# Fetching the first two experts' tokens by rows in a two-layer encoder on one core

## The reference

```
def expert_choice_moe(h, w_router, w_gate, w_up, w_down):
    aff = softmax(xt @ w_router)                 # 256 tokens x 16 experts
    gate, idx = top_k(aff.T, cap)                # cap = 32 tokens per expert
    xe = take(xt, idx, axis=0)
    hid = silu(xe @ w_gate) * (xe @ w_up)        # 1024 -> 1024, per expert
    ye = (hid @ w_down) * gate
    out = zeros_like(xt).at[idx].add(ye)
```

## Time and profile before

| | us |
|---|---|
| median of 3 runs | 1794.33 |
| profiled execution, in all | 1795.57 |
| its span | 1793.8 |
| PE busy | 1645.5 (92%) |
| PEld busy | 781.8 (44%) |
| DVE busy | 516.3 (29%) |
| ACT busy | 461.3 (26%) |
| POOL busy | 67.4 (4%) |
| read from HBM | 446.87 MB |

### The profile page before, as it was taken

One profiled execution on the slowest core, in us unless ns is written; L12 is line 12 of the kernel. 1 busy time (PEld: TensorE's weight loads), 2 busy tenths in 40 slices (PEclk: granted clock), 3 DMA queues, 4 the chain that ended last, 5 costly groups with the idle time before them and its releaser, 6 DMA issues.

```text
span 1793.8 us, 20465 instructions
## 1 busy us (share of the span) xinstructions
PE 1645.5 (92%) x8671; PEld 781.8 (44%) x8671; DVE 516.3 (29%) x999; ACT 461.3 (26%) x1007; POOL 67.4 (4%) x87
## 2 busy tenths in 40 slices
PE   7899799998899979999999999998999988999888
PEld 4454344342243324444445678853443422433233
DVE  3562401121201213255551355543111201112032
ACT  3232211101011105432234565542111110111053
POOL 2000000000000000000004222000000000000000
PEclk9999899999999999999999999999899999999999
DMA  7008269999999994012120000264599999999931
GB/s 247 0 1 328 117 260 427 427 429 427 428 424 428 428 423 176 1 47 94 47 94 1 1 3 2 96 252 193 201 429 427 428 428 428 423 427 429 426 147 47
DMA packets 50906, 450.30 MB, mean 251 GB/s; under 512 B 4931, under 2 KB 7199, under 8 KB 25599
## 3 DMA queue, kind: packets, MB, share of 16 engines
q1 hardware_dynamic: 50288, 448.67, 60.4%
q0 software_dynamic: 288, 0.22, 0.0%
q10 hardware_dynamic: 239, 0.09, 0.0%
HBM read 446.87 MB, written 2.10 MB: 250 GB/s over the span
## 4 chain that ended last, share of the span: by engine, by line
PE 71%; DMA 16%; ACT 4%; DVE 4%; issue 3%; POOL 1%; SPq 1%; DVEq 0%; ACTq 0%; POOLq 0%
PE banks L1722 26%; PE banks L1182 23%; DMA ring<-in_moe_w_up 7%; DMA ring<-in_moe_w_down 5%; PE banks L1373 3%; DMA ring<-in_moe_w_gate 3%; PE banks L1631 3%; PE banks L1701 3%; PE banks L1748 3%; PE banks L1776 2%; PE banks L1342 2%; PE banks L1263 1%; PE banks L1423 1%; PE banks L1401 1%; ACT xn L737 1%
## 5 line engine op out<-in xcount | busy, mean ns | idle before, releaser
L1722 PE MATMUL banks<-ring,misc 128*64 128x512 f32 x2048 | 458.6, 599 | 40.1 <-DMA ring<-in_moe_w_up 23.2
L1722 PEld LDWEIGHTS banks<-ring,misc 128*64 128x64 f32 x2048 | 146.7, 137 | 325.0 <-issue 279.3
L1722 PE MATMUL banks<-ring,hid_t 128*64 128x512 f32 x976 | 218.0, 596 | 17.7 <-DMA ring<-in_moe_w_down 15.1
L1182 PE MATMUL banks<-ring,xt 128*128 128x512 f32 (+1 forms) x448 | 189.8, 585 | 1.1 <-ACT xt L763 0.6
L2354 DVE TENSOR_TENSOR work<-work,banks 128x512 f32<-128x512 f32 x32 | 33.7, 1052 | 483.6 <-PE banks L1722 483.6
L1182 PE MATMUL banks<-xt,ring 128*128 128x512 f32 x384 | 166.7, 594 | 0.0
L1132 ACT ACTIVATE misc<-banks 32x512 f32<-32x512 f32 x64 | 37.5, 586 | 463.1 <-PE banks L1722 462.7
L1722 PEld LDWEIGHTS banks<-ring,hid_t 128*64 128x64 f32 x976 | 68.5, 137 | 157.7 <-issue 136.2
L1182 PEld LDWEIGHTS banks<-ring,xt 128*128 128x128 f32 x448 | 84.8, 190 | 104.0 <-issue 103.0
L1182 PEld LDWEIGHTS banks<-xt,ring 128*128 128x128 f32 x384 | 72.3, 190 | 91.9 <-issue 89.3
L2369 DVE COPY misc<-banks 32x512 f32<-32x512 f32 x64 | 44.2, 691 | 228.2 <-PE banks L1722 227.8
(11 more groups left out here) (311 smaller groups left out, 1532.0 us busy)
## 6 DMA issues: line engine op xcount, KB each, us to landing
ring<-in_moe_w_gate SPq DMA_DIRECT2D x64, 2048.0 KB, 22.3
ring<-in_moe_w_up SPq DMA_DIRECT2D x64, 2048.0 KB, 23.9
ring<-in_moe_w_down SPq DMA_DIRECT2D x58, 2048.0 KB, 25.3
ring<-in_gdn_w_in SPq DMA_DIRECT2D x8, 2048.0 KB, 8.5
ring<-in_ple_w_gate SPq DMA_DIRECT2D x4, 2048.0 KB, 21.5
ring<-in_moe_w_down SPq DMA_DIRECT2D x6, 1024.0 KB, 23.3
ring<-in_mla_w_out SPq DMA_DIRECT2D x2, 2048.0 KB, 23.6
misc<-in_moe_w_down SPq DMA_DIRECT2D x2, 2048.0 KB, 21.3
```

The costliest lines, as they stand in the source:

```text
L1182: mm = pe.matmul(psum[:, banks.bank(st, i), 0:cols], lhs(k), rhs(k), start=(k == 0), stop=(k == n - 1))
L1722: mm = pe.matmul(psum[64 * f:64 * f + 64, bank, :], tokens(4 * kh + k), w[k][:, k, f * HALF:(f + 1) * HALF], start=(kh == 0 and k == 0), s ...
```

## The change

It takes experts 0 and 1 of each layer (called the first and second expert below) out of the first gather.

- `gather_first` makes their tokens *by rows*: the stationary operand is the 32 one-hot columns of one expert, the moving one 512 feature columns of `xn`. The four combinations of sequence s and feature half f go to the four 32-partition groups of one PSUM bank (bank 5 for the first expert, 4 for the second): 8 matmuls for each expert.
- ACT copies each bank to `work` (`hid`, `sg`), TensorE turns it in four 128 x 128 blocks into bank 6 or 7, and DVE multiplies by the gains, an operand spread over the slots, into `xg` (two instructions for each expert). The first gate product waits for the first expert's two, the second gate product for the second's.
- `gather_rest` makes the tokens of experts 2 and 3 with the old layout and 64 moving columns: steps 0 and 1 between the second gate product and the turn of the first hidden block, steps 2 and 3 behind the second up product. Their evictions are placed in the loops of ACT and DVE at `ex` = 1.
- Semaphore totals per layer grow by the new counts (not shown again below).

```diff
+        first_rows = [hid, sg]
...
-                     "gather_in_psum": 4 * NQ, "gather_read_act": 2 * NQ, "gather_read_dve": 2 * NQ,
+                     "gather_in_psum": 4 * NQ + 4, "gather_read_act": 2 * NQ + 2, "gather_read_dve": 2 * NQ + 4,
...
+            L.first_in, L.rows_act, L.rows_dve = (L.done[n] for n in ("gather_in_psum", "gather_read_act", "gather_read_dve"))
+            for n, c in (("gather_in_psum", 4), ("gather_read_act", 2), ("gather_read_dve", 4)):
+                L.done[n] += c
...
-                def gather_out(q):
-
-                    for kp in (0, 2):
+                def gather_first_rows():
+                    for e in range(2):
+                        act.wait_ge(moe_sem["gather_in_psum"], L.first_in + e + 1)
+                        act.activation(first_rows[e], psum[:, 5 - e, :], ACT.Copy).then_inc(moe_sem["gather_read_act"], 1)
+                def gather_out(q, kps=(0, 2), es=slice(0, GRP)):
+                    for kp in kps:
                         act.wait_ge(moe_sem["gather_in_psum"], 4 * q + kp + 1 + L.done["gather_in_psum"])
                         for k in (2 * kp, 2 * kp + 1):
-                            src = psum[:, 6, (k % 2) * 256:(k % 2 + 1) * 256].rearrange("p (s e c) -> p s e c", s=NS, e=GRP)
-                            dst = xg[:, q % 2, k, :, :].rearrange("p e (s c) -> p s e c", s=NS)
+                            src = psum[:, 6, (k % 2) * 256:(k % 2 + 1) * 256].rearrange("p (s e c) -> p s e c", s=NS, e=GRP)[:, :, es, :]
+                            dst = xg[:, q % 2, k, es, :].rearrange("p e (s c) -> p s e c", s=NS)
                             ins = act.activation(dst, src, ACT.Copy, scale=ffn_gain(8 * l + k))
...
-                gather_out(0)
+                gather_first_rows()
                 for ex in range(NE + 1):
...
                         act.activation(sg, psum[:, 2 * (ex % 2), :], ACT.Silu).then_inc(moe_sem["silu_done"], 1)
+                    if ex == 1:
+                        gather_out(0, (0,), slice(2, GRP))
                     if ex:
...
                                        ACT.Copy).then_inc(moe_sem["hid_t_done"], 1)
+                        if ex == 1:
+                            gather_out(0, (2,), slice(2, GRP))
                         if ex % GRP == 2 and ex // GRP + 1 < NQ:
...
                         if ex == PPE + 2:
...
+                def gather_first():
+                    for e in range(2):
+                        for t in range(NT):
+                            for s in range(NS):
+                                for f in range(2):
+                                    g = 32 * (2 * s + f)
+                                    mm = pe.matmul(psum[g:g + 32, 5 - e, :], oh[:, NT * s + t, 32 * e:32 * e + 32],
+                                                   xn[:, NT * s + t, f * HALF:(f + 1) * HALF], start=(t == 0), stop=(t == NT - 1))
+                        mm.then_inc(moe_sem["gather_in_psum"], 1)
+                    for e in range(2):
+                        pe.wait_ge(moe_sem["gather_read_act"], L.rows_act + e + 1)
+                        for b in range(4):
+                            mm = pe.transpose(psum[:, 6 + e, b * P:(b + 1) * P], first_rows[e][:, b * P:(b + 1) * P], ident[:, :])
+                        mm.then_inc(moe_sem["gather_in_psum"], 1)
+                def gather_rest(kps):
+                    for kp in kps:
+                        if kp < 2:
+                            pe.wait_ge(moe_sem["gather_read_dve"], L.rows_dve + 2 + 2 * kp)
+                        else:
+                            who = ("act", "dve")[kp % 2]
+                            pe.wait_ge(moe_sem["gather_read_" + who], 1 + L.done["gather_read_" + who])
+                        for k in range(2):
+                            for s in range(NS):
+                                o = psum[:, 6 + kp % 2, k * 256 + s * P + 64:k * 256 + (s + 1) * P]
+                                c0 = (2 * kp + k) * P
+                                for t in range(NT):
+                                    mm = pe.matmul(o, xn[:, NT * s + t, c0:c0 + P], oh[:, NT * s + t, 64:P],
+                                                   start=(t == 0), stop=(t == NT - 1))
+                        mm.then_inc(moe_sem["gather_in_psum"], 1)
                 def gather(q):
...
                     for kp in range(4):
-                        if q and kp < 2:
+                        if kp < 2:
                             if q >= 2:
...
                             else:
...
-                gather(0)
+                gather_first()
                 for ex in range(NE + 1):
...
                         q, i = ex // GRP, ex % GRP
-                        if i == 0:
+                        if ex < 2:
+                            pe.wait_ge(moe_sem["gather_read_dve"], L.rows_dve + 2 * ex + 2)
+                        elif ex == 2 or i == 0:
                             for who in ("act", "dve"):
...
                         unit_product("gate", ex, 2 * (ex % 2), lambda k: xg[:, q % 2, k, i, :])
+                    if ex == 1:
+                        gather_rest((0, 1))
                     if ex:
...
                         unit_product("up", ex, 2 * (ex % 2) + 1, lambda k: xg[:, q % 2, k, i, :])
+                        if ex == 1:
+                            gather_rest((2, 3))
                         if i == 1 and q:
...
                         if i == 2 and q + 1 < NQ:
...
-                def gather_out(q):
-
-                    for kp in (1, 3):
+                def gather_first_out():
+                    gains_l = ffn_gains[:, :, :].rearrange("p a k -> p (a k)")
+                    for e in range(2):
+                        dve.wait_ge(moe_sem["gather_in_psum"], L.first_in + e + 3)
+                        src = psum[:, 6 + e, :].rearrange("p (b s f c) -> p b s f c", b=4, s=NS, f=2)
+                        for f in range(2):
+                            g = gains_l[:, 8 * l + 4 * f:8 * l + 4 * f + 4].unsqueeze(2).unsqueeze(3).to_broadcast([P, 4, NS, CAP])
+                            dve.tensor_tensor(xg[:, 0, 4 * f:4 * f + 4, e, :].rearrange("p k (s c) -> p k s c", s=NS), src[:, :, :, f, :], g,
+                                              ALU.mult).then_inc(moe_sem["gather_read_dve"], 1)
+                def gather_out(q, kps=(1, 3), es=slice(0, GRP)):
+                    for kp in kps:
                         dve.wait_ge(moe_sem["gather_in_psum"], 4 * q + kp + 1 + L.done["gather_in_psum"])
                         for k in (2 * kp, 2 * kp + 1):
-                            src = psum[:, 7, (k % 2) * 256:(k % 2 + 1) * 256].rearrange("p (s e c) -> p s e c", s=NS, e=GRP)
-                            dst = xg[:, q % 2, k, :, :].rearrange("p e (s c) -> p s e c", s=NS)
+                            src = psum[:, 7, (k % 2) * 256:(k % 2 + 1) * 256].rearrange("p (s e c) -> p s e c", s=NS, e=GRP)[:, :, es, :]
+                            dst = xg[:, q % 2, k, es, :].rearrange("p e (s c) -> p s e c", s=NS)
                             ins = dve.tensor_scalar(dst, src, ffn_gain(8 * l + k), None, ALU.mult)
...
-                gather_out(0)
+                gather_first_out()
                 for ex in range(NE + 1):
+                    if ex == 1:
+                        gather_out(0, (1,), slice(2, GRP))
                     if ex < NE:
...
                         dve.wait_ge(moe_sem["w_used"], piece("up", ex, 1) + 1 + L.done["w_used"])
...
                                           ALU.mult).then_inc(moe_sem["hid_done"], 1)
+                        if ex == 1:
+                            gather_out(0, (3,), slice(2, GRP))
                         if ex % GRP == 1 and ex > GRP:
...
                         if ex % GRP == 2 and ex // GRP + 1 < NQ:
```

## The result

| | before | after |
|---|---|---|
| median | 1794.87 us (6 runs, 1793.71 to 1796.19) | 1801.03 us (6 runs, 1799.91 to 1803.02) |
| ratio | | 1.0036, 95% interval 1.0026 to 1.0046 |
| span of the profiled execution | 1793.8 | 1799.1 |
| expert stage, layer 0 / layer 1 | 443.8 / 444.1 | 446.4 / 446.5 |
| between the stages | 593.8 | 594.6 |

The change makes the kernel slower by 0.36%.

A forecast was written before the change was run, and what follows sets the result against it. The DMA weight stream was taken to bound the expert stages: 7.4 us of added work less 3.0 of lead and 1.9 of slack gives +2.5 per layer, +5.0 in all, 1799.3 us against the 1794.33 median; range 1791.5 to 1803.5.

The forecast's parts named there:

- What bounds the kernel: Expert stages: the full DMA weight queue sets the pace; TensorE matters only where it releases ring slots too late.
- Part 1: Start of each expert stage: the smaller first gather starts the first gate product 3.0 us earlier, bounds 2.2 to 3.4.
- Part 2: TensorE work added inside the expert stage: gather_rest costs 7.4 us per layer, bounds 3.8 and 8.0.
- piece 22: Weight load released by the second expert's down product, behind the gather for experts 5 to 8: tightest release, 4.4 us later.
- the lead: How much earlier the first gate product of each layer starts: 3.0 us forecast.
- Part 3: Sum per expert stage: the latest release comes 4.4 us later, less 1.9 of slack, so +2.5 us per layer.
- the slack of 1.9: Delay that the release of piece 22 can take before the stream runs empty: 1.9 us taken, 1.8 to 2.4.
- three releases: Slot releases compared per stage: the first at -3.0 us, the load issued at 277.80 at 0.2, piece 22 at +2.5.
- A: Expert stages: gather_rest finds slack and the stream keeps the lead, -3.0 us per layer, 1788.3 us; chance 0.12.
- B: gather_rest: 64 moving columns halve its price to 3.8 us, -1.1 us per layer, 1792.1 us; chance 0.10.
- C: First gather: TensorE's clock stays low throughout, the lead is 1.9 us, +3.6 per layer, 1801.5 us; chance 0.08.
- D: First gather: column groups do not run side by side, +13.1 us per layer, 1820.5 us; lesser form 1806.3; chance 0.02.

The follow-up runs named there:

- e1: Changed kernel with the gather for experts 5 to 8 and its evictions one expert later, behind the fourth expert's up product: 1795.21 us, ratio 1.0000 to the kernel before.
- e3: Changed kernel with only a quarter of gather_rest's matmuls, 16 records instead of 64 per layer, some tokens then wrong: 1791.30 us, ratio 0.9972 to the kernel before.
- e6: Kernel before with the matmuls of the gather for experts 5 to 8 made twice, 64 records more per layer: 1808.02 us, ratio 1.0070.
- e9: Kernel before with half the matmuls of the gather for experts 5 to 8 made twice, 32 records more per layer: 1802.29 us, ratio 1.0040.
- e5: Changed kernel with gather_rest behind the first down product, e4's edits, each half of the first gate product awaiting only its own multiplication: 1791.02 us, ratio 0.9975.
- e10: Changed kernel with 128 instead of 64 moving columns in gather_rest's matmuls, the extra ones not read: 1803.00 us, ratio 1.0037 to the kernel before.
- e8: Kernel before with two more 128x512 matmuls (1.72 us) behind the first expert stage, their result overwritten: 1796.60 us, ratio 1.0008.
- e4: Changed kernel with e1's edit and the turn of the one-hot blocks also one expert later, behind the second down product: 1794.76 us, ratio 0.9992 to the kernel before.
- e7: Changed kernel with gather_first's loops turned, each column group's token blocks finished before the next group: 1801.57 us, ratio 1.0032 to the kernel before.
- e11: e5 with the second expert's rows gathered after the first gate product and turned in the middle of the first up product: 1794.77 us, ratio 0.9996 to the kernel before.
- e12: Kernel before with four more 128x512 matmuls (3.43 us) behind the first expert stage: 1798.91 us, ratio 1.0021.

## Why the prediction was right

**What bounds the kernel.** Right. e1, e3, e6 and e9 moved TensorE work in and out at one place, and the stage followed the latest release with a threshold (e1, e6, e9; e3 fits the work as well).

**Part 1.** A lead of 3.4 was measured where 3.0 was forecast, inside the bounds of 2.2 to 3.4. The mis-sized term is the two multiplications: 1.54 us for four, 0.385 each, where I took 0.475 between two other forms; they also began 0.15 us sooner than in the sum (230.83, 6.41 behind the first record, where it has 6.56). Eight rounds took 5.78 (5.8 forecast), the clock rose 4.4 us into the gather, the copies 0.60. What I had wrong in kind is what comes last: the turns of both experts run as one block (230.13 to 231.57), so the second expert's end and the first one's multiplications end together. e5's half wait gave almost nothing because of this.

**Part 2.** Right: two blocks of 3.79, and 7.4 in effect (4.1 later at piece 22, plus the lead of 3.4). e10 shows that it doesn't matter whether 64 or 128 columns move.

**Part 3.** The sum of +2.5 per stage is what came: 2.6 and 2.4. Two errors cancel in it. The lead is 3.4, so piece 22 comes 4.1 later and not 4.4. With the slack of 1.9 that is 2.2, and 2.1 and 2.3 us is what the stream lost net at its two holes. The other 0.1 to 0.5 us come between the second hole and the end of the stage; the sum has no term for them, and why they come is open. That 1.9 came out so well was in part luck. I took 8.6 us for a landing on an empty queue, from one load; in the changed kernel piece 22 lands on one after 7.9 and 8.1, and 10.4 and 10.6 less these would be 2.5, above my bound of 2.4, where the stream shows 1.7 and 1.9. The profile's +5.3 is 5.0 of stages and 0.8 between, less 0.6 ahead of the first gather, and 0.1 at the end. The medians say +6.2, interval 4.7 to 8.3 (0.0026 and 0.0046 of 1794.87); the us above 5.0 is of the size that e8 saw between the stages, but no run ties it to that.
One thing was incomplete. The sum named three releases and left out pieces 15 to 17. In the changed kernel they don't decide, but the queue already runs empty at piece 17; part of e4's miss is the same omission.

**The rivals.** A fell with the landing times of 8 us. It also says what A needs: e3 and e5 are the kernels in which the stream keeps most of its lead, and they were 4 to 5 us faster, not 6. B was settled by e10. C: the low stretch was 4.4 us, after 4.6 before. D: 5.78 us for 32 records is four side by side; the rule of the Trainium skill that would have cost 3.5 us per layer (TensorE: Matmul & The Clock Gate, "The mechanism") is contradicted by L1706 itself.

## What to carry to other kernels

When a stage runs at the pace of a full weight queue, an earlier start is worth only as much as the tightest later slot release allows: read the landing time of each load against that of one on an empty queue (here 8 us), the difference is its slack at most (2.5 us here by the landings, 1.7 to 2.1 by the bytes that the stream failed to move), and look at all of them, not at the two that stand out. Work moved off the start is not free because the queue has a backlog of 29 us later on; where it went, 1.9 us were free, and the same work behind other releases turned +0.36% into -0.25%. Before halving the moving side of a matmul, see whether the weight load has the longer step.

## What the runs showed of the hardware

- Matmuls of different column groups seem to overtake each other. In e7 the program has the four groups' records group by group, four in a row to each, and the engine still ran four side by side: 5.90 us for 32 records, in rounds of four that start 0.85 us apart at 1.2 GHz and 0.43 at 2.4 GHz. The trace doesn't name a record's group, so the overtaking is inferred from the time. The Trainium skill (TensorE: Matmul & The Clock Gate, "The mechanism") has matmuls start and end in strict program order; if that held here, e7's first gather would have taken 10 us or more by the estimate of its expectation.
- A float32 record with 128 stationary columns takes 0.115 to 0.120 us with 64 and with 128 moving columns (3.79 and 3.84 us for 32, changes of shape included).
- TensorE's clock: with a wait of 0.7 us and one of 0.5 ahead of the gate product (e11) it rose 8.4 us behind the first gather record, in the changed kernel 4.4, with no such waits ahead of the product.
- The part between the stages, full of short waits, took 593.8 us; in the slowest of e8's eleven executions, with 1.7 us of work put ahead of it, 600.4, so 4.9 more than the work, at a granted clock of 0.81 instead of 0.89 in one stretch; in e12's profile, with 3.4 us of work, 596.7, so 0.5 less.
- A load of 2 MB that found the queue empty landed after 7.7 to 8.2 us in nearly all cases, one after 8.6. Read against 8 us, the slack at piece 22 would be 2.5; by the bytes moved it was 1.7 to 2.1 (the changed kernel, e6, e9).
